# Constant products in TensorE's waits, and two pieces of work moved, in a two-block transformer kernel

## The reference

```python
h = h + y @ w_out[l]
h = h + cross_attention(rms_norm(h, g_cross[l]), rms_norm(mem, g_mem[l]), w_xq[l], w_xkv[l], w_xo[l])
a = jnp.square(jax.nn.relu(rms_norm(h, g_mlp[l]) @ w_up[l]))
h = h + a @ w_down[l]
```

```python
def rwkv7_step(state, inp):
    r_t, w_t, k_t, v_t, kk_t, a_t = inp
    sk = jnp.einsum('bhij,bhj->bhi', state, kk_t)
    state = (state * w_t[:, :, None, :] - sk[..., None] * (kk_t * a_t)[:, :, None, :]
             + v_t[..., None] * k_t[:, :, None, :])
    y = jnp.einsum('bhij,bhj->bhi', state, r_t)
    return state, y
# after the recurrence, per head:
bonus = jnp.sum(r_h * k_h * r_k, axis=-1, keepdims=True) * v_h
y = (y + bonus) * g
```

## Time and profile before

| | us |
|---|---|
| median of 3 runs | 1565.65 |
| lowest, highest | 1562.19, 1568.24 |
| the profiled execution | 1565.16 |
| its span, first to last instruction | 1563.0 |
| TensorE busy (matmul) | 1477.0 (94%) |
| VectorE busy | 1063.6 (68%) |
| ScalarE busy | 724.0 (46%) |
| GpSimd busy | 306.3 (20%) |
| mean granted TensorE clock | 0.967 |

### The profile page before, as it was taken

One profiled execution on the slowest core, in us unless ns is written; L12 is line 12 of the kernel. 1 busy time (PEld: TensorE's weight loads), 2 busy tenths in 40 slices (PEclk: granted clock), 3 DMA queues, 4 the chain that ended last, 5 costly groups with the idle time before them and its releaser, 6 DMA issues.

```text
span 1563.0 us, 24880 instructions
## 1 busy us (share of the span) xinstructions
PE 1477.0 (94%) x10282; PEld 1323.2 (85%) x10282; DVE 1063.6 (68%) x1814; ACT 724.0 (46%) x1193; POOL 306.3 (20%) x143
## 2 busy tenths in 40 slices
PE   7999899999989778889999999999999999999998
PEld 6887687998877667878999999999998888888886
DVE  5665555665467988453599988999965555555554
ACT  4574444554344434214444454444444444444443
POOL 0046000000045420237799900000000000000000
PEclk9999999999999878779999999999999999999999
DMA  7623433555553300024565554444455666666663
GB/s 272 214 85 133 160 108 114 183 182 196 188 151 104 117 28 2 23 68 136 169 187 174 164 162 150 148 148 143 146 172 162 188 189 188 188 189 189 189 188 121
DMA packets 64879, 235.25 MB, mean 151 GB/s; under 512 B 7424, under 2 KB 7680, under 8 KB 64512
## 3 DMA queue, kind: packets, MB, share of 16 engines
q1 hardware_dynamic: 63904, 231.60, 46.9%
q10 hardware_dynamic: 864, 2.08, 0.4%
HBM read 232.60 MB, written 1.05 MB: 149 GB/s over the span
## 4 chain that ended last, share of the span: by engine, by line
PE 81%; DVE 10%; POOL 3%; ACT 3%; issue 1%; DMA 1%; ACTq 0%; DVEq 0%
PE ps L130 79%; POOL spl L145 3%; PE ps L139 1%; ACT spl L142 1%; DVE spl L145 1%; DVE prep L145 1%; DVE pR L145 1%; DVE pm L145 1%; DMA raw<-in_w_in_a 1%; DVE be L145 1%; DVE pm L154 1%; ACT QK L142 1%; DVE hx L145 1%; DVE junk L145 1%; DMA par<-in_par 0%
## 5 line engine op out<-in xcount | busy, mean ns | idle before, releaser
L130 PE MATMUL ps<-xhl,spl 128*128 128x256 f32 x4944 | 608.5, 283 | 11.3 <-POOL spl L145 9.6
L130 PEld LDWEIGHTS ps<-xhl,spl 128*128 128x128 f32 x4944 | 592.7, 189 | 14.9 <-POOL spl L145 11.2
L142 ACT ACTIVATE spl<-raw 128x1024 fp32r<-128x1024 f32 (+1 forms) x435 | 454.3, 1048 | 320.0 <-PE ps L130 302.0
L145 DVE TENSOR_TENSOR spl<-raw,spl 128x1024 fp32r<-128x1024 f32 (+1 forms) x329 | 402.6, 1229 | 222.7 <-ACT spl L142 220.9
L130 PE MATMUL ps<-spl,Wr 128*128 128x512 f32 x1536 | 358.6, 396 | 3.3 <-DVE Wr L145 3.3
L130 PEld LDWEIGHTS ps<-spl,Wr 128*128 128x128 f32 x1536 | 290.4, 189 | 71.3 <-DVE Wr L145 3.6
L145 POOL TENSOR_TENSOR spl<-raw,spl 128x1024 fp32r<-128x1024 f32 (+1 forms) x106 | 274.4, 2606 | 283.9 <-ACT spl L142 283.4
L142 ACT ACTIVATE Wr<-GE 128x256 fp32r<-128x256 f32 x128 | 53.3, 417 | 183.5 <-PE ps L130 183.5
L142 ACT ACTIVATE GE<-ps 128x256 f32<-128x256 f32 (+42 forms) x176 | 56.9, 326 | 126.6 <-DVE GE L145 109.9
L145 DVE TENSOR_TENSOR Wr<-GE,Wr 128x256 fp32r<-128x256 f32 x128 | 54.4, 426 | 81.2 <-ACT Wr L142 81.2
L130 PE MATMUL ps<-spl,ahl 128*128 128x512 f32 x384 | 90.1, 397 | 0.0
(11 more groups left out here) (337 smaller groups left out, 1236.4 us busy)
## 6 DMA issues: line engine op xcount, KB each, us to landing
raw<-in_eu SPq DMA_DIRECT2D x128, 512.0 KB, 3.6
raw<-in_ev SPq DMA_DIRECT2D x128, 512.0 KB, 4.0
raw<-in_w_up SPq DMA_DIRECT2D x32, 512.0 KB, 3.6
raw<-in_w_down SPq DMA_DIRECT2D x32, 512.0 KB, 4.2
raw<-in_w_in_a SPq DMA_DIRECT2D x16, 512.0 KB, 5.2
raw<-in_w_pq SPq DMA_DIRECT2D x16, 512.0 KB, 3.5
raw<-in_w_rwkv SPq DMA_DIRECT2D x14, 512.0 KB, 3.7
raw<-in_w_in_t SPq DMA_DIRECT2D x8, 512.0 KB, 3.5
```

The costliest lines, as they stand in the source:

```text
L130: return Done(self, self.e and self.e.matmul(out, l, r, start=st, stop=sp))
L142: return Done(self, self.e and self.e.activation(out, a, f, bias=bias, scale=scale, accum_out=acc))
L145: return Done(self, self.e and self.e.tensor_tensor(out, a, b, op))
```

## The change

A new operation `keep(n)` issues n fp32 products of the identity (128x128) with the first 256 columns of the constants (identity and a row of 0 to 127) into a PSUM bank. It writes into the first bank of the queue whose freeing event TensorE has already waited for; where there is none, it waits for the event of the bank at the head. The bank is not taken from the queue, and what is written is overwritten by its next user. `keep` stands with a positive count at 22 places, 131 products in all; every other pair and quad calls it with a count of 0, which only may wait for the bank. The bonus sums go ahead of the transposes of `cn`. TensorE's, ScalarE's and VectorE's `mla()` get one more step ahead of `to_T("ya")`. The wait for GB goes into the loop.

```diff
+    def keep(self, n):
+        free = [b for b, f in self.banks if f is None or self.e is None or self.seen.get(self.table[f][0], 0) >= self.table[f][1]]
+        b, freed = (free[0], None) if free else self.banks[0]
+        if freed is not None:
+            self.wait_ge(*freed)
+        for _ in range(n):
+            self.mm(b[:, 0:256], self.ident, self.still, True, True)
...
-            def pair(inT, tag, W, j, out, key):
+            def pair(inT, tag, W, j, out, key, n=0):
                 for q in range(2):
+                    if q:
+                        pe.keep(n)
...
                 for n, g in RES:
+                    if between and (n, g) == (0, 1):
+                        pe.keep(9)
                     if between and (n, g) == (1, 0):
                         between()
+                        pe.keep(4)
...
+            pe.keep(6)
             to_T("x2", tbs(hB), 8, x_in("h1", 1))
...
+            pe.keep(7)
             for tb in range(2):
                 for hp in range(2):
                     b = pe.bank("pxT", (tb, hp))
...
+            pe.keep(4)
             to_T("x4", tbs(hB), 8, x_in("h3", 1))
...
+            pe.keep(5)
             negated_rows("rw2")
...
-            column_pair("w_rwkv_0", 6, 0)
+            column_pair("w_rwkv_0", 6, 0, 7)
...
+            pe.keep(5)
             for j in range(2):
                 b = pe.bank("nrm", j)
...
             for k in range(8):
+                if k == 3:
+                    pe.keep(13)
                 wh, wl, i = weight("w_mla", k)
...
+            pe.keep(4)
             run(products(0))
-            to_T("c", tbs(cn), 5, x_in("cn", 1))
             b = pe.bank("bon")
...
             pe.give("bon", None, "bon")
+            pe.keep(12)
+            to_T("c", tbs(cn), 5, x_in("cn", 1))
+            pe.keep(3)
...
                     yield
                     yield
+                yield
                 to_T("ya", tbs(yA), 4, lambda tb: pe.wait_ge("ya", tb))
...
-            pe.wait_ge("GB")
+            KEEP = {(1, 0, 0): 3, (1, 1, 0): 4, (1, 1, 1): 5, (2, 0, 0): 11, (2, 0, 1): 4, (4, 1, 1): 3, (5, 0, 0): 5, (5, 1, 1): 3}
             for l in range(1, 6):
                 for j in range(2):
+                    pe.keep(KEEP.get((l, 0, j), 0))
+                    pe.wait_ge("GB")
...
                 for j in range(2):
+                    pe.keep(KEEP.get((l, 1, j), 0))
                     pe.wait_ge("QX", (l, j, 1))
...
             turns.end("k")
+            pe.keep(4)
             for b_ in range(2):
                 b = pe.bank("MV", b_)
...
+            pe.keep(10)
             for c in range(128):
                 apply(c)
...
+                yield
                 to_T("ya", yhA[0], 4, gcols("g_attn_out"))
...
+                yield
                 to_T("ya", yhA, 4, gcols("g_attn_out"))
```

More of the change, by code:

```diff
@@ L92, with __init__ @@
 class Lane:
-    def __init__(self, marks, name, ident, banks, table):
-        self.marks, self.name, self.e, self.seen, self.ident = marks, name, None, {}, ident
+    def __init__(self, marks, name, consts, banks, table):
+        self.marks, self.name, self.e, self.seen = marks, name, None, {}
+        self.ident, self.still = consts
         self.banks = deque((b, None) for b in banks)
@@ L294, in build @@
         ident = C("ident")
+        consts = ident, cst[:, 0:256]
         def whl(i):
@@ L814, in tensor, with column_pair @@
                     pe.give("dn", (tb, g), "h3", (tb, g))
+            pe.keep(4)
             to_T("x4", tbs(hB), 8, x_in("h3", 1))
-            def column_pair(nm, j, f):
-                pair(xT, "x4", nm, j, "col", f)
+            def column_pair(nm, j, f, n=0):
+                pair(xT, "x4", nm, j, "col", f, n)
                 pe.give("col", f, "col", f)
@@ L2643, in build @@
         for name, program in lanes:
-            program(Lane(marks, name, ident, banks, {}))
+            program(Lane(marks, name, consts, banks, {}))
         table, names = dict(marks.at), list(marks.count)
@@ L2651, in lane @@
         def lane(name, e):
-            x = Lane(marks, name, ident, banks, table)
+            x = Lane(marks, name, consts, banks, table)
             x.e = e
```

## The result

| | before | after |
|---|---|---|
| median of 6 runs each, us | 1565.89 | 1571.03 |
| lowest, highest | 1562.19, 1568.24 | 1568.25, 1574.36 |
| the profiled execution, its span | 1565.16, 1563.0 | 1574.36, 1572.2 |
| mean granted clock | 0.967 | 0.980 |

What follows compares the result with a forecast made beforehand. The prediction saw TensorE busy nearly all the time, but at the low clock in twelve stretches (96.0 us) begun after waits. Its terms summed to 2.95 us gained, 1565.2 to 1562.2 us; the range was 1554 to 1570.

Steps and rivals of the forecast that it cites:

- The signs named for "right": w_uq 6 to 8 us later, low stretches gone at five places, some 25 us left behind yA, MV to Ut about 8.
- MV, TAT, Ut (+4.5): At MV to Ut, 10.0 low us on the chain halve, less 0.5 overrun: 4.5 us gained (bounds 0 and 5.1).
- Doubling loop (-0.85 + 1.0): Overruns delay quads and k transposes, 0.85 us lost; VectorE's wait for GK at levels 4 and 5 gives 1.0.
- Bonus sums (-5.9): Sums and 12 products stand behind the bank wait: w_uq 7.3 us later, 1.9 returned, 0.5 more lost; bounds 4 to 9.
- yA one turn later (-0.3): State stage: wait and low stretch stay, yha copies now precede take_u(2): 0.3 us lost (bounds 1 lost, 2 gained).
- hB (+0.6): 6 products before hB's first transposes: 0.6 us gained (bounds -0.8 and 1.7), VectorE's low parts setting w_xq's pace.
- PX (+1.2): 7 products before PX's transposes: first ones 1.2 us late but waiting for last PX anyway; 1.2 us gained (bounds -1.2, 1.7).
- w_o (+0.3): 9 and 4 products in w_o's residual: 1.35 us gained at full clock, 1.1 overrun, 0.3 net.
- The state stage at full clock: Rival: yA's move lets TensorE keep its clock past 656 us, 5.5 us more gained, 1556.7 us; chance 0.13.
- Constants don't hold the clock: Rival: constant products do not keep the clock up, every wait is overrun, nothing comes back, 1584 us; chance 0.05.
- The bonus sums fill the wait: Rival: with a bank free at 539.6, cn's transposes start as before and warm, 1554.4 us; chance 0.12.
- The low stretches did not just move: Rival: low stretches only move to waits left empty, 5 to 8 us of gains gone, 1567 to 1570; chance 0.15.

Runs made afterwards that it cites:

- the moves only: The changed kernel with both moves kept and none of the 131 constant products: 1566.73 us, ratio 1.0016 against the kernel before.
- the turn alone: The kernel before with only yA's transposes one turn later on three engines, no added products: 1566.19 us, ratio 1.0001.
- the loop alone: The kernel before with only the 38 constant products of the doubling loop: 1562.90 us, ratio 0.9984.
- the bonus sums alone: The kernel before with only the bonus sums ahead of cn's transposes and the 12 and 3 products there: 1571.33 us, ratio 1.0037.
- the waits on the path filled: The kernel before with products only at hB, PX, rw2, column pair, norm sums, MV, w_o, last phase; nothing moved: 1559.38 us, ratio 0.9964.
- the kernel with the bank first: The changed kernel, bonus sums' bank taken before the eighth GB product; 5 and 4 products there replace the 12 and 3: 1563.14 us, ratio 0.998.
- path and loop: The kernel before with the products at the waits on the path and the 38 of the doubling loop: 1562.82 us, ratio 0.9979.
- without the 12 and 3: The changed kernel without the 12 products behind the bonus sums and the 3 behind cn's transposes: 1563.70 us, ratio 0.9993.
- the two fitted kernels: On-path products with shortened counts, bonus bank first, 9 loop products, 7 ahead of unmoved yA: 1556.21 us; second adds yA's turn and more products: 1552.93 us.
- fastest kernel: The fitted kernel plus yA's turn and products before x3, in w_mla, before w_uq's banks, state(1) and state(2): 1552.93 us, ratio 0.9924.

## Why the prediction was wrong, step by step

**The step that failed.** The forecast lost 7.3 us up to w_uq's first product and gained 6.05 from there to Ut (1.9 - 0.5 - 0.85 + 1.0 + 4.5). Measured by the means of two traces of each kernel, 8.4 were lost and only 2.1 gained. So the terms from w_uq to Ut are what failed, above all the 4.5 of MV, which one execution had shown, and the doubling loop. To this come the 1.5 us of yA's turn, priced at 0.3, and some 2 us ahead of hB, for which there was no term. The signs named for "right" came nearly all the same (w_uq is 8.3 us later, not 6 to 8): they test where the clock is low, not how long TensorE's chain is.

**MV, TAT, Ut (+4.5): the mechanism is there, the size was one execution's.** MV to Ut is 12.43 us in the trace that was read and 7.58 after. But of six traces of kernels without the four products ahead of MV (the two of before, the moves only, the turn alone, the loop alone, the bonus sums alone) four have 7.65 us there, and the one with the bonus sums 10.88. In the executions of the four the clock fell 7 to 18 us earlier and was back by then, or did not fall at all. From w_uq to Ut, which holds both places, before takes 90.2 and 87.1 us, and with the waits on the path filled 85.8. So the four products are worth 1 to 4 us, by the execution. It also fits that the loop's products gain alone and lose beside them: both keep the clock up into the same stage.

**Doubling loop (-0.85 + 1.0): wrong, in part by its own cascade.** The delay of the first steps was read rightly and mis-sized: from w_uq to the first scaling of QK the changed kernel takes 32.0 us, without the loop's products 30.5, so 1.45 for the 0.85. What it missed is the other end. With the quads warm, TensorE comes to the k transposes while ScalarE still scales: the wait for `ktok` is 0.68 us in before and 2.73 here, empty, and in the four traces that have both the late bonus sums and the loop's products the clock falls there, as it does in the kernel with the bank first. From the first scaling to Ut these five take 54.4 to 54.6 us, without the loop's products it is 52.8. In three others (the loop alone, path and loop, without the 12 and 3) the same wait of 2.73 us leaves the clock up, and it is 52.5 to 53.2. Whether the late bonus sums decide this or chance does is not shown. w_uq to Ut is 86.5 in the changed kernel, 83.3 without the loop's products. Nor does the 1.0 for VectorE's wait for GK show: that wait is 0.47 us in the changed kernel, and 0.46 without the loop's products. And the terms took VectorE and ScalarE for what carries the chain there, as in the kernel before; with the added products TensorE carries it: from 535 to 700 us it holds 47% of the chain of waits before and 81% after.

**Bonus sums (-5.9): right.** 7.3 us were forecast for w_uq's start and 8.3 measured (12 products at 7.55 instead of 7.0, and a wait of 1.40 for the copy of the sums); the return in w_uq was 1.65 of 1.9. Alone the step costs 5.8, on the waits on the path 5.0, and the removal of its 15 products from the whole gives back 7.0.

**yA one turn later (-0.3): mis-sized, beyond its bound of 1 lost.** The text named the cause, `yha` ahead of nU, and took it for almost hidden. The stage is 1.5 us longer in each of the eight traces with the move and no products ahead of state(1) (42.2 us against 40.7 at most). The stretch behind it stayed as forecast, and its end reached into w_o's first quarter, which took 7.77 us instead of 7.05.

**Norm sums (+1.7): right**, 57.56 to 55.84 us. **hB (+0.6): right against the trace that was read only.** From the end of VectorE's last hx to w_xq 2.95 us became 2.36, but the second trace of before, with the clock up there, has 2.14: against it the fill loses 0.2. With 4 products instead of 6 (the two fitted kernels) it is 2.14 as well. **PX (+1.2): wrong.** From the start of VectorE's last PX to the first of the values it was 1.74 us (1.84 in the second trace) and is 1.61, with 4 products instead of 7 1.38: the last four transposes had waited for that PX anyway, and by then the other twelve were done at either clock. **w_o (+0.3): right by the means,** -0.2 by the first traces and +0.4 by the means of two; the second quarter is warm as forecast, 5.96 us. **Last phase (+0.7): right,** +0.6. **Covered fills (0):** right within 1.4 us.

**What no step has.** Up to the end of VectorE's last hx of hB the changed kernel is 6.0 us later by the first traces, of 9.2 in all, and 2.4 us by the second. The programs ahead of hB's transposes differ only in four calls of `keep` with a count of 0, in the pairs of w_in_t, and w_in_t takes 24.22 instead of 24.15 us with them. What differs is the clock. A wait of 2.40 and 2.38 us in the traces of before and of 2.44 in those of after, at 140 to 143 us, is followed by a low stretch in some executions only: in 11 of the 14 traces of kernels with these four calls, and in 1 of the 6 of kernels without. VectorE's last hx of hB ends at 194.0 us in the mean of the 14 and at 192.0 in the mean of the 6. So some 2 us of the miss seem to lie here. Whether the four calls bring them about or chance does is not shown: no run takes the calls out alone. The Trainium skill ("TensorE: Matmul & The Clock Gate", Part 1, What's actually happening) says of a kernel's start that the number of products before the clock rises differs from run to run. Both pairs of traces here show more than that: the places of later falls differ too.

Together, by the means of the two traces of each kernel: w_xq to norm sums 0.4 gained, norm sums to GB 1.7 gained, GB to Ut 6.3 lost (forecast: 1.25 lost), Ut to w_o 1.5 lost, w_o 0.4 and the last phase 0.7 gained. That is 4.6 lost behind w_xq's first product, against 2.35 gained there by the forecast (its 2.95 without hB), and 5.0 of the 6.95 between the two lie between GB and Ut. The 5.9 measured has an interval of 3.8 to 8.1.

**The rivals.** The state stage at full clock did not come, and the reason given against it was right: 3.9 us without a product, and filling them gave 5.9 us where that rival had 5.5. "Constants don't hold the clock" is refuted by every filled wait. "The bonus sums fill the wait" came true only once they had a bank. The low stretches did not just move, their sum fell by a third; but the fall at 601 us is at a wait left empty, as this rival has it. Against the rule on transposes that the forecast took from the Trainium skill ("TensorE: Matmul & The Clock Gate", Part 4: PE-mode transpose) stand the 16 of PX in the changed kernel, 2.04 us right behind the constants, and 10 and 8 in the fastest kernel (543.1 and 650.0 us): all lie in stretches at full clock, and it stays up.

## What to carry to other kernels

An operation moved ahead of a wait fills it only if it can get all its resources there: look at who frees its PSUM bank, and take the bank before the work that empties the queue. Products that hold the clock should be fewer than the wait and stand where TensorE is what comes last. Where they overran it, traces show a part of the overrun as time (hB 2.36 us against 2.14, PX 1.61 against 1.38, the last phase's start 0.6 us later with 10 than with 7). A faster engine turns the next wait into a longer one: 0.68 us became 2.73 at `ktok`, and in w_o the 2.87 us of the kernel before became 5.72 behind 6 products. Before a low stretch is priced, profile the kernel twice: what stands in one trace only is worth a part of its length.

## What the runs showed of the hardware

- The same wait ends at either clock. The wait of 1.23 us ahead of MV was followed by 10 us at the low level, in another execution a wait of 1.36 us was not; the wait of 1.76 us ahead of hB was followed by a low stretch in the first trace of before and not in the second, and behind a wait of 2.73 us for `ktok` the clock fell in five traces and not in three.
- fp32 products of the identity with 256 columns of constants hold the clock, at 0.45 us each at the full level (22 records in 4.91 us).
- The state stage's products, 64 columns wide but for 8 transposes, keep the full clock once it is there (fastest kernel, 646 to 661 us). Where it was lost ahead of them they run at the low level for up to 27 us, and it comes back only behind the start of w_o's wide products. That holds for this stage, not for narrow products as such: in the doubling loop of the changed kernel the clock was back 3.4 us after its fall at 601.9, with 64x64 products (32 records, 1.97 us low, 1.15 full) and transposes alone.
